# Eight tables that set the order of instructions in a mixer stage, replaced by other orders

## The reference, cut to what matters

```python
for i in range(DEPTH):                       # DEPTH = 4
    kind, j = i % N_MIXERS, i // N_MIXERS    # N_MIXERS = 3
    x = x + 0.5 * swiglu(rmsnorm(x, ffn1_norm[i]), ffn1_w_gu[i], ffn1_w_down[i])
    h = rmsnorm(x, mix_norm[i])
    if kind == 0:   m = gated_deltanet(h, ...)          # "GDN", layers 0 and 3
    elif kind == 1: m = stick_breaking_attention(h, ...)
    else:           m = dsa_sparse_attention(h, ...)    # "DSA", layer 2
    x = x + m
    x = x + 0.5 * swiglu(rmsnorm(x, ffn2_norm[i]), ffn2_w_gu[i], ffn2_w_down[i])
```

```python
proj = h @ w_in
qkv = silu(causal_depthwise_conv(proj[..., :3 * GDN_DIM], conv_w))
q = l2norm(q) * GDN_HEAD_DIM ** -0.5;  k = l2norm(k)
g = -exp(a_log) * softplus(a + dt_bias);  beta = sigmoid(b_logit)
g_cum = cumsum(g);  decay = exp(g_cum_i - g_cum_j), lower triangle
lower = where(strict, beta * (k @ k.T) * decay, 0)
sol = triangular_solve(lower + eye, [v * beta, k * beta * exp(g_cum)])
# then, chunk by chunk: u = u_c - w_c @ state; o = q_dec @ state + qk @ u; state = ...
o = rmsnorm(o, norm_g) * silu(z);  out = o @ w_out
```

```python
c_q, c_kv = rmsnorm(proj[..., :384]), rmsnorm(proj[..., 384:640])
q = c_q @ w_uq;  q_idx = partial_rope(c_q @ w_qidx)       # uq and qi below
k, v = c_kv @ w_uk, c_kv @ w_uv                            # uk and uv below
score = sum over h of w_idx[h] * relu(q_idx[h] @ k_idx.T)
idx = top_k(where(causal, score, -inf), 64)
p = softmax(where(mask, q @ k.T * scale, -inf));  out = (p @ v) @ w_out
```

## Time and profile before

| | |
|---|---|
| median of 3 runs | 2908.88 us (2908.8 to 2909.61) |
| the profiled execution | 2909.61 us, span 2907.8 us |
| mean granted TensorE clock | 0.998 |
| TensorE busy | 2878.7 us, 99% |
| VectorE, ScalarE, GpSimd busy | 61%, 54%, 14% |
| memory traffic | 575 MB, mean 198 GB/s |

### The profile page before, as it was taken

How to read it: one execution, slowest core, us unless ns; L and a number is a source line. 1 busy time by engine, 2 the same in 40 slices (tenths; PEclk the granted TensorE clock), 3 DMA queues, 4 the chain that set the end, 5 groups by cost and what they waited for, 6 DMA issues and landing times.

```text
span 2907.8 us, 36498 instructions
## 1 busy us (share of the span) xinstructions
PE 2878.7 (99%) x14543; PEld 2447.9 (84%) x14543; DVE 1782.0 (61%) x2192; ACT 1582.5 (54%) x2006; POOL 412.7 (14%) x636
## 2 busy tenths in 40 slices
PE   9999999999999999999999999999999999999998
PEld 7889988888988888878888899888888888888887
DVE  5558566465566556466556495556675756775664
ACT  5448754444554454565444378544565464566562
POOL 1203312021002112041202105021000010000020
PEclk9999999999999999999999999999999999999999
DMA  8754167676547677537767653386645696645684
GB/s 277 234 191 155 49 213 242 194 243 217 174 154 244 217 221 241 181 116 224 226 207 243 199 159 113 120 244 215 193 155 178 203 276 217 197 155 174 213 285 153
DMA packets 397050, 575.08 MB, mean 198 GB/s; under 512 B 20016, under 2 KB 248624, under 8 KB 396880
## 3 DMA queue, kind: packets, MB, share of 16 engines
q1 hardware_dynamic: 372624, 508.75, 54.8%
q0 software_dynamic: 23680, 62.95, 7.1%
q10 hardware_dynamic: 576, 1.05, 0.1%
HBM read 540.16 MB, written 32.51 MB: 197 GB/s over the span
## 4 chain that ended last, share of the span: by engine, by line
PE 90%; DVE 4%; ACT 3%; issue 1%; DMA 1%; SPq 0%; POOL 0%; DVEq 0%; ACTq 0%
PE ps L430 26%; PE ps L432 26%; PE ps L431 26%; PE ps L616 4%; PE ps L503 1%; PE ps L505 1%; PE ps L504 1%; DVE lo L656 1%; ACT hi L638 1%; DVE qkv L1640 1%; PE ps L587 1%; PE ps L603 1%; ACT qkv L1415 1%; ACT goz L1415 0%; DMA raw<-in_ffn_w_gu 0%
## 5 line engine op out<-in xcount | busy, mean ns | idle before, releaser
L656 DVE TENSOR_TENSOR lo<-raw,hi 128x2048 fp32r<-128x2048 f32 (+3 forms) x473 | 1050.5, 2234 | 450.7 <-ACT hi L638 450.4
L638 ACT ACTIVATE hi<-raw 128x2048 fp32r<-128x2048 f32 (+2 forms) x487 | 907.1, 1871 | 744.2 <-DMA raw<-in_ffn_w_gu 238.2
L430 PE MATMUL ps<-hi,xh 128*128 128x512 f32 (+1 forms) x2208 | 865.6, 392 | 4.0 <-DVE xl L812 2.5
L432 PE MATMUL ps<-hi,xl 128*128 128x512 f32 (+1 forms) x2208 | 858.4, 389 | 0.0
L431 PE MATMUL ps<-lo,xh 128*128 128x512 f32 (+1 forms) x2208 | 857.9, 389 | 0.0
L430 PEld LDWEIGHTS ps<-hi,xh 128*128 128x128 f32 x2208 | 415.0, 188 | 88.6 <-DVE lo L656 5.2
L432 PEld LDWEIGHTS ps<-hi,xl 128*128 128x128 f32 x2208 | 414.9, 188 | 86.2
L431 PEld LDWEIGHTS ps<-lo,xh 128*128 128x128 f32 x2208 | 415.2, 188 | 83.4 <-issue 0.5
L430 PE MATMUL ps<-hi,hhh 128*128 128x512 f32 x704 | 274.6, 390 | 0.0
L432 PE MATMUL ps<-hi,hhl 128*128 128x512 f32 x704 | 273.9, 389 | 0.0
L431 PE MATMUL ps<-lo,hhh 128*128 128x512 f32 x704 | 273.9, 389 | 0.0
(11 more groups left out here) (440 smaller groups left out, 3426.9 us busy)
## 6 DMA issues: line engine op xcount, KB each, us to landing
raw<-in_ffn_w_gu SPq DMA_DIRECT2D x348, 512.0 KB, 4.8
raw<-in_ffn_w_down SPq DMA_DIRECT2D x80, 1024.0 KB, 5.1
raw<-in_w_ff SPq DMA_DIRECT2D x64, 1024.0 KB, 5.6
raw<-in_w_in SPq DMA_DIRECT2D x60, 1024.0 KB, 5.2
raw<-in_gdn_w_in SPq DMA_DIRECT2D x32, 1024.0 KB, 5.8
turned<-hhf POOLq DMA_DIRECT2D x88, 256.0 KB, 4.7
hhr<-turned POOLq DMA_DIRECT2D x352, 64.0 KB, 4.1
raw<-in_sb_w_in SPq DMA_DIRECT2D x12, 1024.0 KB, 5.2
```

Source lines behind the costliest of these rows:

```text
L430: e.matmul(o, a1, r1, start=kk == 0, stop=False)
L432: i = e.matmul(o, a2, r1, start=False, stop=kk == kts - 1)
L638: k.e.activation(k.m.hi[q % RING][:, 0:n], k.m.raw[q % RING][:, 0:n], ACT.Copy).then_inc(*k.up("act_piece_hi", ("hi", q)))
L656: k.e.tensor_tensor(m.lo[i][:, 0:n], m.raw[i][:, 0:n], m.hi[i][:, 0:n].bitcast(F32), ALU.subtract).then_inc(*k.up("dve_piece_lo", ("split" ...
```

## The change

The eight tables are replaced by eight others. Each has the same words as often as before, in another order. No lane, no instruction and no data changes. The diff is eight tables of this kind; here is the one for ScalarE in the DSA stage:

```diff
 DSA_ACT = """
-W W W x1 W p0 W normq W W W turn_q W normq normq p1 W normk turn_q W normk qi turn_q W normk normk W uq index_q
-index_q index index index index index W index W index uv W turn_q uk normk turn_k W attention attention attention
-attention attention attention index W attention attention attention attention attention W W W attention index W W W
-next W W W
+W turn_q W x1 W W p0 normq normq W W W W W turn_q W index_q turn_q normq p1 normk normk W normk W qi uq index_q W W W
+W index normk W index index index index index W uv turn_q uk turn_k attention attention attention W attention
+attention attention W attention W attention attention attention W attention attention normk W W W W index index index
+next W
 """
```

More of the change, by code:

```diff
@@ L1235 @@
 GDN_PE = """
[L1236 to L1239, removed]
+x1 rbc W W nq rbc nk c1 W W W W c0 gates gates W W W W gates W gates W W gates c2 c3 nk nk c0 c2 c3 c1 nk W nk W W c0
@@ L1240 @@
+W W gates kT c3 c1 c2 W W W W W W c2 c3 W W W kT c0 c0 W W c2 c3 c0 c2 nk W nq c0 W c2 c1 nq W c2 nq W c0 c1 rows nq W
+c0 c3 c1 c0 c3 rows c2 qk gates rows c3 rows c1 c0 c2 c1 a0 c3 c1 nq a0 c1 qk c2 c1 a0 a1 c3 a0 c3 a0 qk a0 a1 a1 qk
+a0 a1 a1 a1 W W W a1 W W W W next W
 """
 GDN_ACT = """
-c3 a1 rbc x1 W W W rbc E E ba c0 W W gates E W W W c1 W gates gates W E W nk W E gates W nk nk c2 W nk E c0 nk W c3 c2
-c0 gates W c2 c1 c0 c2 W W E c1 c3 W W c3 c1 a0 E W kT kT W W E W nq E W nq c0 c1 nk E c2 c3 E c0 Z nq c2 c0 nq W nq
@@ L1244 @@
-c1 W sv W c2 gates c0 W W W rows c0 c3 W W rows c1 Z c2 W c3 rows c1 c3 c0 gates c1 c0 c3 c2 W c3 rows gate nq W a0 c1
-c2 c2 a0 c1 a0 a0 a1 a0 c3 a1 a0 W a1 a1 W a1 a1 W next W W W
+rbc c3 x1 W W W rbc a1 E ba W E W gates W W gates W c0 E gates W W c2 E W W nk c1 E W W nk nk nk W c3 c0 W nk E c1 c1
+c0 W c2 W W c0 c1 c2 c3 E W c3 c2 W W E W E W kT nq W E W kT W c0 E c2 c3 E c1 c0 Z W c2 c0 nq W c2 sv nq gates gates
+nq c0 Z c2 nq rows c3 c3 c1 c2 gates c2 W c0 W W c0 rows a0 rows c1 c3 rows c0 c1 W c1 c1 W c3 gate c3 a0 W c2 c1 a0
@@ L1246 @@
+a0 W a0 nk gates nq c3 a1 a1 a0 a0 a1 W W a1 a1 a1 W W W next W
 """
 GDN_DVE = """
[L1248 to L1251, removed]
+x1 rbc W clear W W E c2 E c3 nk gates nk W c1 c0 W W gates W W gates E E gates W W W E gates W gates W W nk c0 c3 c2
@@ L1252 @@
+nk c1 E c0 nk nk W c3 W nq c1 c2 c0 E W W inv c0 E W W E c3 W c1 W W E c2 inv E E c0 c2 W W c2 nq c2 nq c0 c2 nq c0 nq
+W c1 W nq c3 c0 c3 c3 c1 gates c0 W W c3 c2 c1 qk c2 c1 a0 c1 c1 W c3 W a0 qk a0 a1 c3 W c1 W a0 c0 a0 W qk a1 a0 a1
+c3 qk W a1 a0 a1 a1 a1 W W W out W next out out W rbc W c2 W
 """
 GDN_POOL = """
-clear c1 W c2 W W c0 c1 c2 c3 c3 c3 W W W c0 c1 c2 c2 c1 W W c1 W W c0 W W W W inv c2 W c0 W W c2 c0 W c3 W c0 W W W
-c3 c2 inv c3 W W c2 W c1 W c1 W W W W c1 c1 c1 c0 W W c3 c2 W c1 W W c3 c0 c3 W c0 c0 c2 W c0 W W W W c2 c3 c3 W
+W W c0 c0 W clear W c1 W W W c3 W W c2 c3 c1 c0 W c1 c2 W W W c1 c1 W c1 W W W W W W c0 inv c3 W c1 W inv c0 W W c1 W
@@ L1256 @@
+W c2 c0 c2 c3 c1 c3 W W c2 c1 c1 c3 c2 W c0 c2 c3 c3 W W c0 c3 W c3 W W W c3 W c0 c2 c2 c2 W W W W W c2 c0 c0 W
 """
@@ L2178 @@
 DSA_PE = """
-turn_q normq W normq x1 W W turn_q W W normk W W normq W W W W normk W normk turn_q normk W W index_q W normk index_q
-index index index index index W W W turn_q W turn_k index attention attention attention attention attention attention
-W attention attention W index index index attention attention attention W attention W W W next W W
+normq turn_q W index_q x1 W W W normk W W normq W W normq W W W turn_q normk W normk W turn_q W W normk normk index_q
+index W index index index turn_q W W W turn_k attention attention attention attention attention attention attention W
@@ L2182 @@
+attention index attention index index W index attention attention W attention W index W W next W W
 """
 DSA_ACT = """
-W W W x1 W p0 W normq W W W turn_q W normq normq p1 W normk turn_q W normk qi turn_q W normk normk W uq index_q
-index_q index index index index index W index W index uv W turn_q uk normk turn_k W attention attention attention
-attention attention attention index W attention attention attention attention attention W W W attention index W W W
-next W W W
+W turn_q W x1 W W p0 normq normq W W W W W turn_q W index_q turn_q normq p1 normk normk W normk W qi uq index_q W W W
@@ L2188 @@
+W index normk W index index index index index W uv turn_q uk turn_k attention attention attention W attention
+attention attention W attention W attention attention attention W attention attention normk W W W W index index index
+next W
 """
 DSA_DVE = """
-normk x1 W normq W W normq W W W W W normq W normk W W normk normk index_q normk W turn_q W W index turn_q index index
-index index index W index W index index attention attention attention W attention attention W attention W turn_q
-attention attention attention attention index_q attention attention W out W W W W next out turn_q out W W W
+normq x1 W W W W normq W normk W W W normq W normk W W W normk normk index_q normk turn_q turn_q turn_q index index_q
@@ L2193 @@
+index index index W index W index index index index attention attention W attention W W attention attention turn_q
+attention attention attention W W attention attention attention W attention W out W W W out next out W W W
 """
 DSA_POOL = """
-W W W W W W W W W W W W W attention W W W attention attention attention attention attention attention W attention
-attention W attention W attention W W W attention W W W W W
+W W W W attention W W W W W W W W W W W W W W attention attention attention W attention attention attention attention
@@ L2197 @@
+attention W attention W W W W W W attention W attention
 """
```

## The result

The changed kernel takes 2940.84 us in the median of 4 runs (2939.73 to 2942.58), against 2908.84 for the kernel before: the ratio is 1.0112, with a 95% interval of 1.0095 to 1.0131. I had predicted 2913.4 and a range of 2908 to 2919. The profiled execution took 2943.33 us.

The account below looks back on a forecast made before the run. It took TensorE's matmuls to bound the kernel, with about 29 us of holes. DSA +3.3 us and both GDN stages +1.2 us gave 2914.1 from the profiled run, 2913.4 by the median; range 2908 to 2919.

Parts of the forecast that it names:

- ScalarE's part: DSA stage: three splits now stand between the dqiT copy and the first relu, 5.1 us in all.
- the relu's bank: DSA stage: TensorE's q transposes need banks that the relus of heads 4 to 7 read, +1.0 us.
- ahead of `uk`: DSA stage: TensorE waits 1.75 us before the uk product for banks that ScalarE's dqT copies read late.
- one of 0.85: DSA stage: an attention step ahead of the output product leaves TensorE waiting for GpSimd's fourth head, +0.85 us.
- the walk of the DSA stage: DSA timeline followed through ScalarE, TensorE and VectorE: late relus and uk +2.5, attention +0.85, output step −0.1, sum +3.3 us.
- The gate wait: GDN stages: the two gate transposes stand right behind the matmuls they read from and wait for ScalarE's copy, +0.65 us.
- the old wait at the queries: GDN stages: wait of 0.8 us, taken as 1.0, goes because the sum of query squares moves behind more matmuls.
- the 0.5 us at the key squares: GDN stages: the sum of key squares loses its cover of 24 matmuls and waits for ScalarE's second input, +0.5 us.
- the first chain group: GDN stages: two chain groups whose banks are still being read, estimated together at +0.35 us a stage.
- The clock rival: Longer, more broken stretch before 1274 brings the half clock sooner or doubles it, +1.3 to 4 us, 2915.9; chance 0.12.
- The ScalarE-bound rival: GDN stages before the apply steps: ScalarE runs out of its 3.6 us, +2.5 a stage, about 2918 us; chance 0.16.
- That the change is hidden, or gains: Two rivals: delays covered, 2908 to 2910 us, chance 0.14; old waits go and none come, 2902 to 2903.5, chance 0.08.

Follow-up runs that it names:

- after_fill: Changed kernel with GpSimd filling lo with zeros instead of subtracting for its weight pieces: 2915.58 us in one run, DSA stage 90.02, GDN stages 185.44 each.
- before_early: Kernel before with ScalarE's hi splits 216 and 217 moved ahead of the eight relus in the DSA stage: 2916.32 us, DSA stage 94.25.
- before_lo: Kernel before with VectorE's lo split of uk moved behind the scoring, ahead of the top-k: 2915.12 us, DSA stage 95.58.
- gdn_inv: Changed kernel; GpSimd's first GDN split waits for VectorE's split 49; second stage, VectorE fills zeros for pieces 46 to 48: second stage 186.47 us.
- gdn_inv2: gdn_inv with VectorE's transpose of the finished inverse moved ahead of convolution group E.10 in the second GDN stage: that stage 185.38 us, the first 187.09.
- gdn_tables: Kernel before with only the four GDN tables changed, DSA tables old: 2927.79 us, ratio 1.0071.
- dsa_undo3: Changed kernel with splits 216 and 217 behind the relus, the uk split ahead of scoring, and GpSimd's old DSA table: DSA stage 92.21 us.
- better: Kernel before with two swaps in TensorE's GDN table, moving a query-square sum and an apply step behind twelve matmuls: 2912.3 us, ratio 1.0016.

## Why the prediction was wrong, by its steps

*ScalarE's part held.* 5.1 us of splits ahead of the relus: 5.09. In after_fill, where little is held, the waits of my walk stand at their places: 0.67 us for the relu's bank (forecast 1.0), 1.18 ahead of `uk` (1.75), and two of 0.37 and 0.21 at later attention heads where I had put one of 0.85. DSA without the hold: +2.45 us, forecast +3.3. How close that is stays open: the stage of before ran at 0.98 of the clock and that of after_fill at 1.00, which by the prediction's own estimate is up to 1.5 us, so like for like the growth lies between 2.5 and 4.

*The step that failed* is the one in the walk of the DSA stage where I let the eighth relu start "by VectorE's pace of scoring (12 instructions in 4.13 us, two a head)". That pace is a reading of a stretch in which GpSimd was idle: its first split came at 1257.47, behind L2455. The change moved the `hi` splits that release GpSimd ahead of the relus, and I followed these splits on ScalarE only. A step that is moved takes along what it releases. GpSimd was counted at its attention steps only. The same omission stands in the other sum: 1.75 us of `uk` split between scoring and mask were counted as 1.75. before_early and before_lo show each of the two moves alone at +6.7 and +8.0 us. The GDN sum has it a third time: VectorE's split of piece 49 is in it at nothing, and beside a GpSimd split it took 6.25 us instead of 2.3. The hold in sum, with the clock that followed it: 11.5 us in DSA, 8.3 and 8.0 in the GDN stages. By one of the prediction's own signs it is wrong: a GDN stage moved by 11.5 us, where 2 was the limit. The other sign asked only that the DSA stage grow by 2 us from `dqiT` to the first scores; it grew by 9.6 (31.9 instead of 22.3), against the 2.5 of the walk.

*The GDN terms.* The gate wait was forecast at 0.65 and is 0.47; the old wait at the queries did go, and the 0.5 us at the key squares did not come. Two came that I had missed or made small. VectorE's split of piece 47 stands 6.7 us later (277.13 instead of 270.43 in the old stage) and TensorE waits 0.84 for it, where I had 0.15. And the first chain group, 0.35 in my sum, waits 1.5, since VectorE's transpose of the inverse comes late. In the changed kernel it starts as soon as GpSimd has the inverse:

```profile
287.06 1.25 DVE L1756 STREAM_TRANSPOSE gow<-goz 128x1024 f32<-128x1024 f32 x1 [0.81 <-POOL goz L1834]
```

With the inverse 5.9 us sooner, in gdn_inv, it came only 0.6 us sooner in its stage, behind E.10, whose input ScalarE writes behind a split. So two things hold this place, and gdn_inv2, which frees both, took 1.7 us off the stage (187.09 to 185.38). Without GpSimd's subtractions a GDN stage is +3.2, not +0.6: 0.47, 0.83 and 1.56 less the old 0.82 make 2.0 of it, and the other 1.2 are not traced. VectorE's hold on GpSimd's inverse is still in these 3.2. The apply steps wait 1.23 for `vb` (2.56 us instead of 0.69), beside a GpSimd split; this went in after_fill.

*The rivals.* The clock rival named a real effect, 1.6 to 2.9 us per GDN stage, but as a consequence of long holes; it was no cause. The ScalarE-bound rival is refuted for the bulk of the loss: with the hold gone and ScalarE's lists unchanged, 8 us per GDN stage went. Of the 3.2 that stayed, the 1.5 at the chain group hang in part on E.10, which waits for ScalarE, so some of it may be this rival's; no run separates it. That the change is hidden, or gains, is out.

*The range* of 11 us was built from the terms of one walk. No bound in it came from asking which engines would now run side by side that had not before.

## What to carry to other kernels

When instructions move, list for each engine what it will now run beside each other engine, not only what it waits for; a duration from a trace holds for the neighbours it had there. Here VectorE and GpSimd must not overlap with instructions of two on-chip inputs: a long one that has begun costs a short one all of the time that it still has to run. In this kernel, whose TensorE is 99% busy, the two small holes that I tried to fill were the cover of something else, and moving work into them brought back larger ones.

## What the runs showed of the hardware that I had not expected

L2447 with one input and float32 data, VectorE's TENSOR_SCALAR, is held as well, even by a fill on GpSimd (1.72 us for the pair instead of 0.54), while L2454 with two inputs runs freely beside a fill and is held by a subtraction (0.28 against 4.67). The top-k rounds kept their times (MAX8, L2460, and MATCH_REPLACE8, L2463: 0.27 to 0.41 us) in the four runs where GpSimd's splits ran beside them: before, gdn_tables, dsa_undo3 and better. Copies out of a bank (L1686, 0.68 us) kept theirs beside a split too. Short instructions are held one split each, in turns (4.70 and 4.66 us in before_lo). And GpSimd is held in the same way by VectorE's splits: steps of 0.4 us took 2.3, in the old order one of them and in the changed order three a stage.
